# Where the picks of a PEER layer are added: all picks of the second token half in the table matrix, 12 gathered vectors of the first half on VectorE, four table tiles requested before the last dot products

## The chip, the cores and the metric

The kernel runs on one core of one Trainium2 chip. The metric is the device time of one execution in microseconds (us). Engines are called by the profile's names: PE is TensorE, DVE is VectorE, ACT is ScalarE, POOL is GpSimd (here it only issues gathers) and SP is SyncE (here it only issues plain DMAs).

## The reference

A transformer block of 256 tokens with a width of 2048, followed by a second block whose last part is a PEER layer and a final norm. Only that last part matters here:

```
q = (x @ w_q).reshape(B, S, PEER_HEADS, 2, PEER_HALF)          # 8 heads
s = einsum('bshpk,hpnk->bshpn', q, sub_keys)                   # 128 keys on either side
...                                                            # top 16 of the 256 best sums per head
act = gelu(einsum('td,tkd->tk', xt, expert_u[ids])) * g        # 8 x 16 = 128 picks a token
out = einsum('tk,tkd->td', act, expert_v[ids])                 # tables: 16384 experts x 2048
h = h + out ; return rms_norm(h, final_norm_g)
```

## The kernel before

The tokens lie on the 128 partitions, in two halves (t = 0 and t = 1) of 128 tokens. A plan (`Plan`) keeps a rough clock for each engine and writes one list of steps; each engine walks that list and takes its own steps, so it sets the order on each engine. Ahead of the PEER layer lies a stream of projections; the part that the change touches begins at some 2200 us of the run.

**Dots.** For pick n (0 to 127 are those of the first half, 128 to 255 those of the second), POOL gathers one row of `peer_u` a token (`get_u`, L3210, 128 x 8 KB = 1.05 MB) into one of up to six buffers `Ub`, and DVE multiplies and sums it (`dot`, L3071). `U_SETS` says which buffers a pick may use: two leave the ring before the end, and the last 20 dots use `Ub2` to `Ub4`. Each four dots pass a gelu on ACT (L2364) and a product on DVE (`weigh`, L3078), which gives the activations `dots[t]`. Top-k work for the second half lies between the dots of the first.

**Upper 1024 columns of the output.** For the first half, POOL gathers the upper half of a row of `peer_v` for each pick (`get_v`, L3225, 128 x 4 KB = 0.52 MB), ACT makes a diagonal matrix of the activations (L2370) and PE adds the product in the banks M0 and M1 (`spread`, L1920): 128 vectors. 102 of them use a ring of 16384 bytes and one buffer more (`Vx`) or early places (`Vb`), the last 26 four buffers `Vy`. `EARLY_ROWS` lets 106 be requested early; the other 22 come when the dots of pick 236 are due. For the second half, DVE adds the gathered vector times the activation to X (`aside`, L3126): 128 of them.

**Lower 1024 columns.** These go through a dense product with the whole table. For each half, 32 groups (`one_hot`, `spike`, `build`, `keep`) make a 128 x 16384 matrix A[t]: two factors made of one-hot rows, multiplied on PE (`build`, L1943, four products of 128 x 128), copied from the banks T0 and T1 by ACT (`keep`, L2436). The second factor, `spikes`, is made by DVE in four of five groups (L3093) and by ACT in the groups with i % 5 == 1 (L2390, L2393, L2429). In the second half's matrix there are only the first 112 picks (`BUILT`); the last 16 (`LATE`) are added by DVE as 16 more asides of the lower columns, through the indices `vlow`. The last 16 dots are held and lie between the spikes of the second half's matrix, as do the last 22 spreads between the builds.

**Dense stage.** SP loads 128 tiles of `peer_v` (128 rows x 1024 columns, 0.52 MB, L1615), after all spreads, into five places, the fifth free only after the last build. ACT makes a high part (`high`, L2450) and an fp32r copy of the matrix's column (L2456), DVE the low parts of both (L3104, L3111), and PE multiplies (`mul`, L1947, twelve products for a tile). Each eighth tile is not split and goes to PE as fp32, in four products of four passes. The 144 asides lie between the tiles' low parts on DVE. `rows` (L3117) adds M0 and M1 to X, `upper` norms the upper columns, `close` the rest.

Of the kernel before, what the change touches and what calls it, by code (L numbers as in the profile page):

```python
# [15 lines left out]
P = 128  # L16
# [284 lines left out]
class Plan:  # L301
# [642 lines left out]
    def place_free(self, m):  # L944
# [4 lines left out]
        if m >= FIRST_ROWS:  # L949
            return self.when(("chosen", 1, 7)) if NE - 1 in self.spreads else None  # L950
# [42 lines left out]
    def make(self):  # L993
# [22 lines left out]
        yield lambda: None if FIRST_ROWS - 1 not in self.spreads else self.when(("chosen", 1, 7), ("xn", 1, 3))  # L1016
# [6 lines left out]
        yield lambda: self.acted.get(BUILT // GROUP + 31)  # L1023
        self.add("turn_act", 1)
        self.put("ACT", 0.6, self.put("PE", 0.4, 0.0))
        for i in range(32, 64):
            yield lambda: c["ACT"] if on_act(i) else c["DVE"]
            self.add("spike", i)
            self.put("ACT" if on_act(i) else "DVE", 3.3 if on_act(i) else 1.05, 0.0)
            self.build(i)  # L1030
            self.spiked = i - 31
        self.keep(63)

    def products(self):
# [3 lines left out]
        self.spiked = 0  # L1038
# [4 lines left out]
        while self.row_next < 128 or self.ranks.get("weigh", 0) < 256 // GROUP or want:  # L1043
# [18 lines left out]
            if m < 128 and m in self.v_in and m // GROUP in self.acted and m - EARLY_ROWS < 0.75 * self.spiked:  # L1062
# [2211 lines left out]
```

## Time and profile before

| | us |
|---|---|
| runs | 3372.7, 3373.82, 3377.07 |
| median | 3373.82 |
| the profiled execution | 3378.8 |
| its span | 3376.9 |
| dots with full DMA queues, second half | 2600 to 2879 |
| matrix of the second half, with 16 dots and 22 spreads | 2880 to 2965 |
| dense stage, first to last product | 2973.45 to 3364 |
| close | 3364 to 3376.9 |

In a view by stretches, each engine's busy time stands with the number of its instructions in brackets; the last three columns are the clock granted to PE as a share of 2.4 GHz, the busy share of the DMA engines and what they moved. In a list of instructions, the brackets at a row's end say how long the engine stood idle ahead of it and what ended that.

### The profile page before, as it was taken

The page shows a single profiled execution, that of the slowest core. Times are in us where ns is not written, and L with a number is a line of the kernel's source. Part 1 is how long each engine was busy: PE and PEld are TensorE (multiplying, and loading weights), DVE is VectorE, ACT ScalarE, POOL GpSimd, SP SyncE. Part 2 cuts the span into 40 slices and gives each one's busy share as a digit, 9 for nine tenths or more (in the row PEclk, how much of TensorE's full clock was granted, in tenths as well). Part 3 has the DMA queues.
Part 4 walks back from the last instruction along what each step waited for, and adds up shares of the span by engine and source line. Part 5 has one row for each costly group of instructions (what it writes and reads, how often), then busy time and mean ns, then how long its engine had stood idle before and what let it go on. Part 6 is the DMA issues. An engine that isn't in the chain of part 4 may idle for free.

```text
span 3376.9 us, 37646 instructions
## 1 busy us (share of the span) xinstructions
PE 2935.7 (87%) x14064; PEld 2381.0 (71%) x14064; DVE 2590.2 (77%) x3926; ACT 1671.3 (49%) x2698; POOL 597.3 (18%) x549
## 2 busy tenths in 40 slices
PE   8999999999999999999999999986653420789998
PEld 7998998888888888888888888842221320567776
DVE  7786777775557787876557685799889999778987
ACT  6554556554445555554445763133444765444444
POOL 0000000000000000000000000655544333335552
PEclk9999999999999999999999999998876555899999
DMA  6554555555555555556556567999999999889997
GB/s 235 163 150 156 163 170 174 175 163 200 190 182 187 181 192 184 188 181 209 187 188 228 163 203 271 356 380 417 422 403 402 427 427 424 326 325 364 389 369 281
DMA packets 426647, 877.50 MB, mean 260 GB/s; under 512 B 18811, under 2 KB 249116, under 8 KB 392928
## 3 DMA queue, kind: packets, MB, share of 16 engines
q1 hardware_dynamic: 347208, 453.16, 40.3%
q0 software_dynamic: 78240, 421.56, 31.2%
q8 instruction: 112, 1.84, 0.2%
q14 instruction: 71, 0.58, 0.0%
q10 hardware_dynamic: 1016, 0.35, 0.0%
HBM read 872.91 MB, written 2.10 MB: 259 GB/s over the span
## 4 chain that ended last, share of the span: by engine, by line
PE 71%; DMA 12%; DVE 11%; issue 2%; POOL 2%; ACT 2%; DVEq 0%; POOLq 0%; ACTq 0%
PE W L1773 14%; PE W L1781 11%; PE W L1783 11%; PE W L1782 11%; DMA Ub<-in_peer_u,ids 8%; PE W L1771 7%; PE W L1947 7%; DVE Ub L3071 5%; DMA Vr<-in_peer_v 2%; DMA Vx<-in_peer_v,vid 2%; PE M L1920 2%; PE M L1834 1%; DVE X L3126 1%; POOL Ub L3210 1%; PE W L1707 1%
## 5 line engine op out<-in xcount | busy, mean ns | idle before, releaser
L2630 DVE TENSOR_TENSOR wl<-raw,wh 128x1024 fp32r<-128x1024 f32 (+1 forms) x720 | 850.9, 1187 | 562.7 <-ACT wh L2079 561.0
L2079 ACT ACTIVATE wh<-raw 128x1024 fp32r<-128x1024 f32 (+1 forms) x720 | 740.7, 1031 | 893.7 <-PE W L1783 573.9
L1773 PE MATMUL W<-u,wh 128*128 128x512 f32 x2040 | 722.3, 397 | 0.0
L1771 PE MATMUL W<-u,wl 128*128 128x256 f32 x2176 | 603.0, 282 | 0.2 <-DVE u L2592 0.2
L3071 DVE CUSTOM_DVE_ANT_0 Ub<-Ub,W 128x2048 f32<-128x2048 f32 x227 | 516.1, 2284 | 39.1 <-DMA Ub<-in_peer_u,ids 29.3
L1773 PEld LDWEIGHTS W<-u,wh 128*128 128x128 f32 x2040 | 383.3, 188 | 88.2
L1781 PE MATMUL W<-wh,u 128*128 128x512 f32 (+1 forms) x1152 | 436.2, 379 | 1.2 <-DVE u L2990 1.0
L1783 PE MATMUL W<-wh,u 128*128 128x512 f32 (+1 forms) x1152 | 427.9, 371 | 0.0
L1782 PE MATMUL W<-wl,u 128*128 128x512 f32 (+1 forms) x1152 | 427.6, 371 | 0.0
L1771 PEld LDWEIGHTS W<-u,wl 128*128 128x128 f32 x2176 | 410.7, 189 | 6.4 <-issue 0.5
L3210 POOL DMA_INDIRECT Ub<-in_peer_u,ids x256 | 262.0, 1023 | 394.7 <-DVE dots L3071 268.4
L1920 PE MATMUL M<-Vx,diag 128*128 128x512 f32 x360 | 190.3, 682 | 110.7 <-DMA Vx<-in_peer_v,vid 82.5
L1781 PEld LDWEIGHTS W<-wh,u 128*128 128x128 f32 x1152 | 216.5, 188 | 30.7 <-issue 1.4
L1783 PEld LDWEIGHTS W<-wh,u 128*128 128x128 f32 x1152 | 216.2, 188 | 30.6
L1782 PEld LDWEIGHTS W<-wl,u 128*128 128x128 f32 x1152 | 216.6, 188 | 29.0
L1920 PEld LDWEIGHTS M<-Vx,diag 128*128 128x128 f32 x360 | 75.0, 217 | 225.3 <-issue 173.0
L3237 POOL DMA_INDIRECT side<-in_peer_v,vid x128 | 174.7, 1365 | 169.0 <-DVE X L3126 152.5
L1943 PE MATMUL T<-spikes,AA 128*128 128x128 f32 (+1 forms) x512 | 101.2, 363 | 98.2 <-issue 88.3
L3126 DVE SCALAR_TENSOR_TENSOR X<-side,dots,X 128x1024 f32<-128x1024 f32 x144 | 184.3, 1280 | 2.5
L1943 PEld LDWEIGHTS T<-spikes,AA 128*128 128x128 f32 (+1 forms) x512 | 91.5, 265 | 118.7 <-issue 118.7
L1947 PE MATMUL W<-Vh,Ah 128*128 128x512 f32 x448 | 148.0, 411 | 25.4 <-DVE Al L3111 25.3
L3104 DVE TENSOR_TENSOR Vl<-Vr,Vh 128x1024 fp32r<-128x1024 f32 x112 | 137.0, 1223 | 37.9 <-ACT Vh L2450 36.0
(401 smaller groups left out, 4711.4 us busy)
## 6 DMA issues: line engine op xcount, KB each, us to landing
raw<-in_w_in SPq DMA_DIRECT2D x128, 1024.0 KB, 5.2
raw<-in_w_up SPq DMA_DIRECT2D x88, 1024.0 KB, 4.9
Vr<-in_peer_v SPq DMA_DIRECT2D x128, 512.0 KB
raw<-in_w_down SPq DMA_DIRECT2D x44, 1024.0 KB, 5.0
raw<-in_w_in SPq DMA_DIRECT2D x144, 256.0 KB, 3.4
raw<-in_w_out SPq DMA_DIRECT2D x32, 1024.0 KB, 5.0
raw<-in_w_proj_a SPq DMA_DIRECT2D x16, 1024.0 KB, 4.9
Wb<-in_peer_w_q SPq DMA_DIRECT2D x16, 1024.0 KB, 6.7
```

The lines of the kernel that those rows point to most:

```text
L1771: i = q.matmul(pr[h][:, 0:T], vl, xh, start=False, stop=False)
L1773: i = q.matmul(o, vh, u[:, :, kk, :], start=False, stop=last)
L1781: q.matmul(o, th, H[:, k, :], start=first, stop=False)
L1782: q.matmul(o, th, L[:, k, :], start=False, stop=False)
L1783: i = q.matmul(o, tl, H[:, k, :], start=False, stop=last)
L1920: i = q.matmul((M0, M1)[j][:, :], diag[:, m % 4, :], Vb[slot][:, CK[j]], start=m == 0, stop=m == 127)
L1947: return q.matmul(banks[f"W{2 * t + c}"][:, :], left, right, start=j == 0 and k == 0, stop=j == 127 and k == 2)
L2079: q.activation(wh[:, s % NS, 0:b.half], r, ACT.Copy).then_inc(s_hi, 1)
L2630: q.tensor_tensor(wl[:, s % NS, 0:b.half], r, wh[:, s % NS, 0:b.half].bitcast(F32), SUB).then_inc(s_lo, 1)
L3071: q.tensor_tensor_reduce(U[:, :], U[:, :], inputs[:, :], 1.0, 0.0, MUL, ADD, dots[t][:, k:k + 1]).then_inc(s_dot, 1)
L3126: q.scalar_tensor_tensor(X[:, 1, c], side_b[i % NA][:, :], dots[1][:, k:k + 1], X[:, 1, c], MUL, ADD).then_inc(s_aside, 1)
L3210: q.indirect_dma_start(Ub[place][:, :], None, eu, bass.IndirectOffsetOnAxis(ids[t][:, k:k + 1], 0)).then_inc(s_u[place], 16)
```

## The change

The second half's matrix takes all 128 picks (`BUILT`, `LATE` and `vlow` go). The asides of the lower columns go; in their place the first half's last 12 gathered vectors are added by DVE, so that there are 140 asides, 14 of which (`AMID`) lie between the spikes of the second half. PE spreads 116 vectors (`ROWS`), all through the five-place ring, none held. No dot is held either: all 256 lie ahead of the second half's spikes, and the last 20 use four buffers. The ring of spikes has four places instead of six. SP may request four table tiles when 248 dots are done and all picks are chosen. The high and low part of tile 0 lie ahead of the last four builds, and `rows` ahead of the first spike.

```diff
 HALF = D // 2
-LATE = 16
-BUILT = 128 - LATE
 NE = 12
-NB = 4
-FIRST_ROWS = 102
-EARLY_ROWS = 106
+ROWS = 116
...
-ASIDES = 128 + LATE
+ASIDES = 256 - ROWS
+AMID = 14
...
-NP = 6
-U_SETS = ((48, (0, 1, 2, 3)), (206, (0, 1, 2, 3, 4, 5)), (236, (0, 2, 3, 4, 5)), (256, (2, 3, 4)))
+NP = 4
+U_SETS = ((48, (0, 1, 2, 3)), (206, (0, 1, 2, 3, 4, 5)), (236, (0, 2, 3, 4, 5)), (256, (2, 3, 4, 5)))
...
-    if i < 128:
-        return i, 1
-    return BUILT + i - 128, 0
+    return (0, ROWS + i) if i < 128 - ROWS else (1, i - 128 + ROWS)
...
-        yield lambda: self.acted.get(BUILT // GROUP + 31)
+        yield lambda: self.acted.get(63)
         self.add("turn_act", 1)
         self.put("ACT", 0.6, self.put("PE", 0.4, 0.0))
+        self.add("rows")
+        self.put("DVE", 1.3, 0.0)
+        for i in range(ASIDES):
+            self.add("get_aside", i)
...
+            while self.beside < min(AMID, (i - 33) // 2):
+                self.put("DVE", 1.3, 0.0, "aside", self.beside)
+                self.beside += 1
+            if i == 59:
+                self.put("ACT", 1.05, 0.0, "high", 0)
+                self.put("DVE", 1.22, 0.0, "low", 0)
         self.keep(63)
...
-            if dot is not None and n >= 128 + BUILT and self.spiked < 2 * (n - 127 - BUILT):
-                dot = None
...
-            v_free = self.place_free(v) if v < (EARLY_ROWS if n < 124 + BUILT else 128) and v // 16 < self.chosen else None
+            v_free = self.place_free(v) if v < ROWS and v // 16 < self.chosen else None
...
-            while a < min(ASIDES, (j - 1) * ASIDES // 120):
+            while a < min(ASIDES, self.beside + (j - 1) * (ASIDES - self.beside) // 120):
...
-            e.wait_ge(s_spread, 128)
+            e.wait_ge(s_gw, 16)
+            e.wait_ge(s_dot, 248)
             for j in range(128):
                 if j == 4:
                     e.wait_ge(s_built, 64)
```

The last dots on POOL, before: each gather of `peer_u` (`Ub`) has a gather of a vector (`Vy`) near it.

```order
L3225 DMA Vy_271<-in_peer_v,vid_194 128x1024
L3210 DMA Ub_169<-in_peer_u,ids_193 128x2048
L3225 DMA Vy_272<-in_peer_v,vid_194 128x1024
L3225 DMA Vy_273<-in_peer_v,vid_194 128x1024
L3210 DMA Ub_168<-in_peer_u,ids_193 128x2048
```

And now, the last four gathers of `peer_u` and the first asides:

```order
L3202 DMA Ub_168<-in_peer_u,ids_193 128x2048
L3202 DMA Ub_167<-in_peer_u,ids_193 128x2048
L3202 DMA Ub_169<-in_peer_u,ids_193 128x2048
L3202 DMA Ub_170<-in_peer_u,ids_193 128x2048
L3226 DMA side_230<-in_peer_v,vid_194 128x1024
L3226 DMA side_231<-in_peer_v,vid_194 128x1024
```

The 16 gathers are no longer spread through the stage of the second matrix; they lie in one row ahead of it.

On DVE, the start of the second half's spikes, before:

```order
L3078 TENSOR_TENSOR dots_191<-dots_191,gw_185 128x4
L3093 TENSOR_SCALAR spikes_208<-wide_206,idT_202,actT_204 112x128 x4
L3093 TENSOR_SCALAR spikes_209<-wide_206,idT_202,actT_204 112x128 x4
L3071 ISA Ub_167,dots_191<-Ub_167,W 128x2048
L3071 ISA dots_191 128x1
L3093 TENSOR_SCALAR spikes_210<-wide_206,idT_202,actT_204 112x128 x4
```

And now, with the last dot ahead of it:

```order
L3062 ISA Ub_170,dots_191<-Ub_170,W 128x2048
L3062 ISA dots_191 128x1
L3069 TENSOR_TENSOR dots_191<-dots_191,gw_185 128x4
L3108 TENSOR_TENSOR X<-M,X 128x512 x2
L3084 TENSOR_SCALAR spikes_207<-wide_205,idT_201,actT_203 128x128 x4
L3084 TENSOR_SCALAR spikes_208<-wide_205,idT_201,actT_203 128x128 x4
L3084 TENSOR_SCALAR spikes_209<-wide_205,idT_201,actT_203 128x128 x4
L3084 TENSOR_SCALAR spikes_210<-wide_205,idT_201,actT_203 128x128 x4
L3117 SCALAR_TENSOR_TENSOR X<-side_230,dots_190,X 128x1024
```

The dots between the spikes have gone ahead; `rows` and asides have come in.

On PE, the first builds of the second half, before (`T<-spikes` is a build, `M<-Vy` a spread):

```order
L1933 MATMUL T<-ident,dots_191 112x128
L1943 MATMUL T<-spikes_208,AA 128x128 x4
L1920 MATMUL M<-Vy_270,diag 128x512 x2
L1943 MATMUL T<-spikes_209,AA 128x128 x4
L1920 MATMUL M<-Vy_271,diag 128x512 x2
L1943 MATMUL T<-spikes_210,AA 128x128 x4
```

And now:

```order
L1926 MATMUL T<-ident,dots_191 128x128
L1935 MATMUL T<-spikes_207,AA 128x128 x4
L1935 MATMUL T<-spikes_208,AA 128x128 x4
L1935 MATMUL T<-spikes_209,AA 128x128 x4
L1935 MATMUL T<-spikes_210,AA 128x128 x4
L1935 MATMUL T<-spikes_207,AA 128x128 x4
```

No spread is left between the 32 builds.

## Rows read from the trace of the kernel before

**Rows 1.** Stretches: start:end length, busy (count) of PE, PEld, DVE, ACT, POOL; PEclk, DMA, GB/s.
```profile
2600.00:2850.00 250.00, 65.95 (x258) 57.35 (x258) 236.13 (x232) 174.47 (x484) 93.66 (x100) 0.50 1.01 427
2880.00:2965.00 85.00, 73.88 (x345) 48.97 (x345) 62.82 (x139) 43.70 (x112) 34.52 (x37) 0.93 0.85 316
2973.40:3364.00 390.60, 373.62 (x1472) 278.07 (x1473) 346.13 (x370) 166.37 (x244) 190.99 (x139) 0.99 0.93 352
```

**Rows 2.** The same view, three stretches around the end of the first half's dots.
```profile
2530.00:2540.00 10.00, 10.00 (x23) 4.13 (x21) 7.79 (x9) 7.63 (x20) 5.86 (x7) 0.97 0.98 385
2550.00:2560.00 10.00, 0.00 (x0) 0.00 (x0) 9.69 (x22) 3.23 (x8) 1.88 (x3) 0.50 0.91 365
2560.00:2570.00 10.00, 3.18 (x4) 1.51 (x5) 10.00 (x10) 6.84 (x21) 6.74 (x8) 0.50 0.91 334
```

**Rows 3.** Instructions in order of time, POOL: start us, us, engine, line, operation.
```profile
2863.70 0.93 POOL L3225 DMA_INDIRECT Vy<-in_peer_v,vid  x1 [0.30 <-issue]
...
2868.67 0.94 POOL L3210 DMA_INDIRECT Ub<-in_peer_u,ids  x1 [0.30 <-issue]
```

**Rows 4.** The same view, DVE: pick 239's dot and the first spikes.
```profile
2877.02 2.29 DVE L3071 CUSTOM_DVE_ANT_0 Ub<-Ub,W 128x2048 f32<-128x2048 f32 x1 [4.73 <-DMA Ub<-in_peer_u,ids]
...
2880.88 1.38 DVE L3093 TENSOR_SCALAR spikes<-wide,idT,actT 112x128 f32<-112x128 f32 x5 [1.10 <-ACT actT L2384]
```

**Rows 5.** The same view, PE, builds of the second half.
```profile
2882.14 2.04 PE L1943 MATMUL T<-spikes,AA 112*128 112x128 f32 x8 [1.78 <-DVE spikes L3093]
...
2902.07 1.95 PE L1943 MATMUL T<-spikes,AA 112*128 112x128 f32 x16
...
2939.42 1.95 PE L1943 MATMUL T<-spikes,AA 112*128 112x128 f32 x16
...
2944.43 2.05 PE L1943 MATMUL T<-spikes,AA 112*128 112x128 f32 x8 [3.06 <-ACT spikes L2429]
2946.28 2.77 PE L1920 MATMUL M<-Vy,diag 128*128 128x512 f32 x3
```

**Rows 6.** The same view, ACT, around the wait of 3.06 us.
```profile
2940.51 0.60 ACT L2436 ACTIVATE AA<-T 128x512 f32<-128x512 f32 x1 [2.02 <-PE T L1943]
...
2943.06 1.28 ACT L2429 ACTIVATE spikes<-spikes,actT 112x128 f32<-112x128 f32 x4
```

**Rows 7.** Stretches of 2.5 us in which the granted clock changed, and one in which not.
```profile
2885.00:2887.50 2.50, 2.50 (x13) 1.51 (x12) 2.50 (x11) 0.11 (x1) 0.53 (x1) 0.87 0.04 16
2892.50:2895.00 2.50, 1.15 (x10) 0.99 (x10) 2.28 (x10) 2.30 (x7) 1.56 (x2) 1.00 0.91 315
2942.50:2945.00 2.50, 0.57 (x3) 0.60 (x3) 0.00 (x0) 2.47 (x7) 0.00 (x0) 0.74 0.97 357
2950.00:2952.50 2.50, 2.50 (x12) 1.74 (x12) 2.50 (x4) 0.60 (x1) 1.87 (x2) 0.90 0.25 41
2977.50:2980.00 2.50, 2.50 (x12) 2.02 (x11) 1.04 (x2) 0.42 (x1) 0.81 (x1) 0.94 0.40 59
```

**Rows 8.** PE in order of time: the dense stage's first product and two later places.
```profile
2973.45 1.19 PE L1947 MATMUL W<-Vh,Ah 128*128 128x512 f32 x2 [8.49 <-DVE Al L3111]
...
3119.27 0.70 PE L1947 MATMUL W<-Vh,Ah 128*128 128x512 f32 x2 [0.66 <-DVE Al L3111]
...
3132.99 3.59 PE L1947 MATMUL W<-Vr,Ar 128*128 128x512 f32 x8
...
3136.02 1.03 PE L1947 MATMUL W<-Vh,Ah 128*128 128x512 f32 x2
```

**Rows 9.** Who waited for whom, PE in 3000:3364: total us, times, longest.
```profile
PE W L1947 <- DVE Al L3111: 16.5, 14, 2.5
```

**Rows 10.** Groups of DVE, 2965:3377: count, busy us, mean ns, idle before.
```profile
L3126 DVE SCALAR_TENSOR_TENSOR X<-side,dots,X 128x1024 f32<-128x1024 f32 x144 | 184.3, 1280 | 2.5
L3104 DVE TENSOR_TENSOR Vl<-Vr,Vh 128x1024 fp32r<-128x1024 f32 x112 | 137.0, 1223 | 37.9 <-ACT Vh L2450 36.0 <-issue 1.5
L3111 DVE TENSOR_TENSOR Al<-AA,Ah 128x256 fp32r<-128x256 f32 x112 | 46.9, 419 | 5.5 <-ACT Ah L2456 5.2
```

More of the change, by code:

```diff
@@ L155, in landings @@
     count, table = [0] * NE, {}
-    for kind, n, place in ("row", 128, row_sem), ("aside", ASIDES, lambda i: i % NA):
+    for kind, n, place in ("row", ROWS, row_sem), ("aside", ASIDES, lambda i: i % NA):
         for i in range(n):
@@ L1015, in make @@
         self.keep(31)
-        yield lambda: None if FIRST_ROWS - 1 not in self.spreads else self.when(("chosen", 1, 7), ("xn", 1, 3))
+        yield lambda: None if ROWS - 1 not in self.spreads else self.when(("chosen", 1, 7), ("xn", 1, 3))
         self.add("turn_ids", 1)
@@ L1028, in make @@
             self.add("spike", i)
-            self.put("ACT" if on_act(i) else "DVE", 3.3 if on_act(i) else 1.05, 0.0)
+            self.put("ACT" if on_act(i) else "DVE", 3.3 if on_act(i) else 1.15, 0.0)
             self.build(i)
-            self.spiked = i - 31
+            while self.beside < min(AMID, (i - 33) // 2):
[4 more added lines that the diff above has]
+                self.put("DVE", 1.22, 0.0, "low", 0)
         self.keep(63)
@@ L1042, in products @@
         since = 0
[L1043 removed]
+        while self.row_next < ROWS or self.ranks.get("weigh", 0) < 256 // GROUP or want:
             m = self.row_next
@@ L1103, in dense @@
     def dense(self):
-        for i in range(ASIDES):
-            self.add("get_aside", i)
-        a = 0
+        a = self.beside
         for j in range(128):
-            self.add("high", j)
-            self.add("low", j)
-            if j == 0:
-                self.add("rows")
-            while a < min(ASIDES, (j - 1) * ASIDES // 120):
+            if j:
+                self.add("high", j)
+                self.add("low", j)
+            self.add("column", j)
+            while a < min(ASIDES, self.beside + (j - 1) * (ASIDES - self.beside) // 120):
                 self.add("aside", a)
@@ L1421, in program @@
         Vb += [ring_x] + [at(f"Vx{i}", [HALF], END - 16384 + 4096 * i) for i in range(NX - 1)]
-        Vb += [at(f"Vy{i}", [HALF], Z + 16384 + 4096 * i) for i in range(NB)]
         wide_x = ctx.enter_context(nc.psum_tensor("W", [P, D], F32))
@@ L1942, in build @@
                 for x in range(4):
-                    m = q.matmul((T0, T1)[i % 2][:, col(x)], A[t][0:k, g, x * P:x * P + P], spikes[spike_place(i)][0:k, x, :], start=True, stop=True)
+                    m = q.matmul((T0, T1)[i % 2][:, col(x)], A[t][:, g, x * P:x * P + P], spikes[spike_place(i)][:, x, :], start=True, stop=True)
                 m.then_inc(s_built, 1)
@@ L2502, in scalar @@
                   "copy_xn": copy_xn, "top_exp": top_exp, "gelu": gelu, "spread": spread, "turn_ids": turn_ids, "turn_act": turn_act,
-                  "one_hot": one_hot, "spike": spike, "keep": keep_group, "high": high, "upper": upper, "close": close})
+                  "one_hot": one_hot, "spike": spike, "keep": keep_group, "high": high, "column": column, "upper": upper, "close": close})
         def vector(q):
```

92 lines of the change are left out of this document (40 added, 52 removed).

## The prediction

> **What bounds the kernel now.** Only the run behind 2500 us is touched, so I read the view by stretches first. It shows three stages with three bounds [rows 1]. From 2600 to 2850 the DMA engines are full (share 1.01, 427 GB/s) while DVE is busy for 236 of 250 us: the dots come as fast as their rows do. From 2880 to 2965 (second matrix, with 16 dots and 22 spreads among it) DMA falls to 316 GB/s and PE is busy for 74 of 85 us. From 2973.4 to 3364 (dense stage) PE is busy for 373.6 of 390.6 us and DVE for 346. The second view is the list of waits: in the dense stage PE waits 14 times for DVE's `Al`, 16.5 us in all [rows 9]. The third is the list of instructions in order of time, for the paces below.
>
> Two prices recur. A gather of `peer_u` is 128 x 8 KB = 1.049 MB, at 427 GB/s 2.46 us of full DMA; a gathered half row or a table tile is half of that, 1.23 us [rows 1].
>
> **The change, part by part**, in absolute times of the profiled execution.
>
> *Pick 239's dot.* It starts at 2877.02 after a wait of 4.73 us for its row, and ends at 2879.3 [rows 4]. That row was requested at 2868.67, behind four gathers for `Vy`, the first at 2863.70 [rows 3]. The changed order has none there, so I take the whole wait off: 2874.6. The bounds are 0 and 4.7, and it is nearest to the latter, since four times 1.23 us is 4.9.
>
> *Ten more vectors early.* 116 of them go ahead of the second half's dots instead of 106. They are requested between picks 110 and 143, in the neighbourhood of 2530 to 2620, and would cost 10 x 1.23 = 12.3 us if DMA had been full. It was not quite: in three stretches of 10 us it moved 385, 365 and 334 GB/s [rows 2], which leaves (42 + 62 + 93) / 427 x 10 = 4.6 us. I take 7.7 us; bounds 3 (a queue filled at all other places too) and 12.3. ACT's ten diagonals and PE's ten spreads hide there: PE is busy for 66 of 250 us [rows 1]. On POOL each gather waits for the spread five vectors earlier, and gathers of `peer_u` are queued behind it. PE's queue holds a few of these spreads behind first-half builds, which wait for ACT; that is why I don't go below 7.7.
>
> *The 16 dots that were held.* They lose their place in the matrix stage and stand ahead of it, at the pace of DMA: 16 x 2.46 = 39.3 us. DVE's 2.2 to 2.3 us for a dot hides in it. With four buffers, a row has 4 x 2.46 = 9.8 us for its round of request, landing and dot, and the one requested at 2868.67 took 8.35 us to its dot's start while four vectors were in its way [rows 3, 4]; 8.35 + 2.3 is 10.7, without the vectors well below 9.8, so the buffers don't bind. The Trainium skill, "DMA: Bandwidth & Descriptors", section "Anatomy of one DMA — SWDGE (gpsimd) path", fits a lone gather as 2.0 us plus its bytes at 436 GB/s, which is 4.4 us for this one; by it an idle queue would make the round 6.7 us and the sum would be the same. No run here shows a lone one.
>
> *Four tiles early.* SP requests them when 248 dots are done, so they share the DMA engines with the last gathers: 4 x 1.23 = 4.9 us. I take 4, with bounds 0 and 4.9. Together the last dot ends at 2874.6 + 7.7 + 39.3 + 4 = **2925.6**.
>
> *The second matrix, without dots and spreads.* What is late next is ACT. Every fifth group's spikes are made there, and it starts them only after it has copied the group two earlier. The trace shows that pattern once without spreads in the gap: PE starts two builds at 2939.42, ACT copies at 2940.51, its spikes end at 2944.3, and PE starts the next build at 2944.43 after standing idle for 3.06 us [rows 5, 6]. So from the build two groups ahead to the one that waited are 5.0 us. Then three builds lead to the same point of the next round. At full clock they cost 0.9 each (two take 1.95, of which the last 1.06 is one build [rows 5]), some 2.75 with the first; a round is 7.8 us. At half clock the first one takes 1.85 until the next instruction starts (2944.43 to 2946.28 [rows 5]), three 5.5; a round is 10.5.
>
> Which clock is it? In the stretch of that idle the granted clock fell (0.74), and it was back only in the stretch from 2950 (0.90); after an idle of 1.35 us around 2893 it stayed at 1.00 [rows 7]. A mean of 0.87 in the stretch from 2885, 0.90 from 2950 and 0.94 from 2977.5 puts the returns to 2.4 GHz at 2885.6, 2950.5 and 2977.8, so 3.5, 6.1 and 4.3 us after PE had started again at 2882.14, 2944.43 and 2973.45 [rows 5, 7, 8]; mean 4.6. In 4.6 us, 2.5 builds are done at 1.83, and the rest of three takes 0.45: a round is 5.0 + 5.05 = 10.05 us. PE stands idle for 3.06 us in every round now, since nothing fills the gap, so I take this for all. The Trainium skill says in "TensorE: Matmul & The Clock Gate", section "HAM oscillation — how this bites in real kernels", that a loop whose every batch of products waits for its next operand pays the restart at low clock each time and not once; it speaks against this change, the trace agrees in its one such gap, and the other way round (full clock) is a rival below.
>
> The stage then is: last dot to first build 2.8 (2879.3 to 2882.14 [rows 4, 5]) plus `rows`, two adds of some 0.65 = 4.1; two builds and the third's whole 2.05 at half clock, 5.7; copy 0.5, ACT's spikes 3.3: some 13 with the signals, 12.5 if the clock is back for the third. Five rounds (groups 36 to 61) 50.2. From group 61's build to the last copy and through the matrix's first column on ACT and DVE 6.3: builds 4.7, and 1.6 for 0.5 + 0.4 + 0.42 and signals. Sum **69 us**; with all rounds at full clock 12.5 - 1 + 39 + 4.6 = 55, and at half throughout, where the part of 5.0 grows to 5.9, 78. DVE hides: in a round it has four spikes of 1.03 and 2.8 asides of 1.28, 7.7 us.
>
> The first product starts at 2925.6 + 69 = 2994.6. Before it was 2973.45, 8.49 us after PE's last build, waiting for the first tile, its high and its low part [rows 8]. That wait is gone, and it is in the sum: tile 0 is prepared during the builds.
>
> *The dense stage.* For eight tiles DVE has seven pairs of low parts and 9.6 asides (144 over 120 tiles). By busy time, which overlaps by 0.08 from one to the next: 7 x (1.14 + 0.34) + 9.6 x 1.2 = 21.9 us [rows 10]. PE needs 13.72 / 5 = 2.74 for a split tile and 3.03 for an unsplit one, 7 x 2.74 + 3.03 = 22.2 [rows 8]. That tie makes the waits. Afterwards 14 asides are done earlier: 126 are left, 8.4 for eight tiles, DVE 20.4 us. DMA is relieved alike, from 17.6 to 16.4 transfers in eight tiles. PE then bounds alone. The ceiling is the 16.5 us [rows 9], plus what low clock costs: a mean of 0.99 over 390.6 us is up to 8 us at 1.2 GHz, half of it lost, 2.2 of these 4 at the start, where they stay [rows 1, 7]. So 16.5 + 2 = 18.5; I take **18**, and as the other bound 6: DVE relieved by 1.5 us in 22, while waits for late tiles remain (`Vl` waited 36.0 us for ACT's high part [rows 10]). 390.6 - 18 = 372.6, hence 3367.2; the close of 12.9 us stays: 3380.1.
>
> That is 3.2 us more than the span of 3376.9. The profiled execution of 3378.8 would be 3382.0; it lies 5.0 above the median of the runs, 3373.8, so I put the prediction at 3373.8 + 3.2 = **3377.0**.
>
> **The rivals.**
> *PE's clock stays full between the builds.* The stage takes 55 and not 69 us: 3363, faster. For it: the only gap of this kind had its drop, but it is one gap. Against: ACT's order makes the 3.06 us in each round.
> *It stays at half for the whole stage.* Slower: 78 instead of 69 us, 3386. The place is the 32 builds; it decides once the stage takes over 72.6 us, which is when more than some five of the builds that I count at full run at half. For it: first-half builds ran at 0.50 from 2600 on [rows 1]. Against: they had 26% busy PE there.
> *The dense stage gains 6 and not 18.* Its waits come from late tiles and not from DVE's load: 3389.
> *The change doesn't delay the last dot so much*: vectors in gaps (3) and tiles for nothing (0): 3368.
>
> **How the numbers follow.** A measurement of this kernel can tell some 0.2%, 6.7 us. Forecast 0.55, with its own range 3369 to 3385: 0.38 within 6.7 us, 0.12 slower, 0.05 faster. Full clock 0.15, faster. Half clock 0.12, slower. Dense stage 0.10, slower. Earlier last dot 0.08: 0.03 faster, 0.05 the same. Faster 0.23, the same 0.43, slower 0.34. The range reaches from full clock to half clock and nearly to the dense rival: 3362 to 3388.
>
> **What would show it.** The last dot's end near 2926 (below 2920: vectors and tiles were hidden). From there to the first dense product 69 us, and in it six idle times of PE near 3 us with a granted clock between 0.5 and 0.8; a mean near 1.0 proves the first rival. In the dense stage PE's waits for `Al` under 3 us in total and 370 to 375 us from first to last product. The prediction fails if POOL stands for several us behind a spread between 2560 and 2620, or if asides come too late between the spikes, so that DVE's spikes and not ACT's end PE's waits.

## The result and the profile after

The changed kernel takes 3381.9 us (median of 20 runs, 3376.35 to 3385.24); the kernel before, run beside it, 3374.35 us (20 runs, 3371.71 to 3378.29). The ratio is 1.002, with a 95% interval of 1.0014 to 1.0027: slower by 7.5 us or 0.2%, little, but outside the interval of no change. The forecast was 3377.0, 3.2 us slower than before; the time lies within its range. One of the six runs of e10_best_98 below took 13281 us; its ratio leaves that run out, and the median of the other five is 3364.1 us.

The profiled execution took 3378.09 us, with a span of 3376.3. The view by stretches (columns as in [rows 1]) has the stage of the dots, 60 us of the new matrix stage, and the dense stage from its first to its last product:

```profile
2600.00:2850.00 250.00, 72.36 (x275) 57.90 (x275) 231.06 (x228) 176.62 (x491) 95.76 (x102) 0.53 1.01 427
...
2925.00:2985.00 60.00, 37.59 (x251) 35.90 (x252) 49.22 (x125) 37.49 (x87) 17.90 (x19) 0.84 0.54 167
...
2987.60:3365.40 377.80, 370.74 (x1480) 277.17 (x1480) 326.07 (x355) 168.01 (x250) 159.80 (x121) 1.00 0.92 340
```

The first is that of [rows 1] with more spreads on PE. The second is new: PE is busy for 63% of the time, DVE for 82%, and the DMA engines are half idle. No engine is full, so a wait sets the pace. The third is shorter than before. Measured alike, from the first product to the end of the last, the dense stage took 2973.45 to 3366.12 = 392.7 us before and takes 2987.62 to 3365.36 = 377.7 now. (The prediction let it end at 3364 before, two microseconds short; its gain isn't touched by that.)

**The dots.** POOL's instructions in order of time (columns as in [rows 3]) show the first and the last of the last four vectors for PE. They are requested while the first half's dots end and behind them; the dot of pick 128 starts at 2603.45:

```profile
2601.80 1.09 POOL L3214 DMA_INDIRECT Vx<-in_peer_v,vid  x1 [0.30 <-issue]
...
2627.86 0.93 POOL L3214 DMA_INDIRECT Vx<-in_peer_v,vid  x1 [0.31 <-issue]
```

DVE, pick 239's dot (first line; before, [rows 4]) and five of the last eight dots:

```profile
2880.06 2.29 DVE L3062 CUSTOM_DVE_ANT_0 Ub<-Ub,W 128x2048 f32<-128x2048 f32 x1
...
2902.49 2.29 DVE L3062 CUSTOM_DVE_ANT_0 Ub<-Ub,W 128x2048 f32<-128x2048 f32 x1 [0.21 <-DMA Ub<-in_peer_u,ids]
2904.92 2.29 DVE L3062 CUSTOM_DVE_ANT_0 Ub<-Ub,W 128x2048 f32<-128x2048 f32 x1
2907.97 2.29 DVE L3062 CUSTOM_DVE_ANT_0 Ub<-Ub,W 128x2048 f32<-128x2048 f32 x1 [0.75 <-DMA Ub<-in_peer_u,ids]
2911.71 2.29 DVE L3062 CUSTOM_DVE_ANT_0 Ub<-Ub,W 128x2048 f32<-128x2048 f32 x1 [1.44 <-DMA Ub<-in_peer_u,ids]
...
2924.59 2.29 DVE L3062 CUSTOM_DVE_ANT_0 Ub<-Ub,W 128x2048 f32<-128x2048 f32 x1
```

Up to 2904.92 they stand 2.4 to 2.6 us apart, the time of their rows at 427 GB/s. SP issues the four tiles at 2902.35, and the next five each come 3.05 to 3.74 us after the one ahead. The last one ends at 2926.9.

**The matrix.** PE in order of time, from the first build to the first dense product (before, [rows 5, 8]):

```profile
2929.69 5.66 PE L1935 MATMUL T<-spikes,AA 128*128 128x128 f32 x32 [1.77 <-DVE spikes L3084]
2938.38 4.95 PE L1935 MATMUL T<-spikes,AA 128*128 128x128 f32 x40 [3.03 <-ACT spikes L2419]
2946.27 6.45 PE L1935 MATMUL T<-spikes,AA 128*128 128x128 f32 x40 [2.94 <-issue]
2955.66 4.95 PE L1935 MATMUL T<-spikes,AA 128*128 128x128 f32 x40 [2.94 <-issue]
2963.55 6.45 PE L1935 MATMUL T<-spikes,AA 128*128 128x128 f32 x40 [2.94 <-issue]
2972.94 3.93 PE L1935 MATMUL T<-spikes,AA 128*128 128x128 f32 x32 [2.94 <-issue]
2979.94 1.13 PE L1935 MATMUL T<-spikes,AA 128*128 128x128 f32 x8 [3.07 <-DVE spikes L3084]
2981.37 4.50 PE L1935 MATMUL T<-spikes,AA 128*128 128x128 f32 x24 [0.30 <-issue]
2987.62 0.70 PE L1939 MATMUL W<-Vh,Ah 128*128 128x512 f32 x2 [1.75 <-DVE Al L3102]
```

Eight instructions are one build; x40 are the five of a round. There are the six idle times near 3 us that the prediction named. Five of them stand ahead of a group whose spikes ACT makes. The sixth, at 2979.94, is another: it stands behind DVE, which waited for ACT's high part of tile 0 (below), and the last group of ACT's, at 2981.37, waits for 0.30 us only. The rounds alternate: from build to build of the same place they take 7.89 and 9.39 us. Two stretches of the first view, a short round and the long one behind it, tell why (the granted clock is the column after the busy times: 1.00, then 0.82). The last two stretches lie in the long round, the first 0.8 us of its builds and what follows:

```profile
2938.40:2946.30 7.90, 4.96 (x41) 4.70 (x41) 7.68 (x19) 6.04 (x15) 2.76 (x3) 1.00 0.64 196
2946.30:2955.70 9.40, 6.46 (x41) 6.25 (x41) 7.26 (x20) 6.03 (x15) 1.92 (x3) 0.82 0.47 124
2946.27:2947.07 0.80, 0.80 (x7) 0.80 (x8) 0.13 (x1) 0.38 (x1) 0.08 (x1) 1.00 0.27 20
2947.10:2950.50 3.40, 3.40 (x18) 3.40 (x17) 2.31 (x5) 1.20 (x2) 0.37 (x1) 0.51 0.48 152
```

The clock is full during the pause and when PE starts again. It falls 0.8 us later, with PE at work, and PE works through the whole stretch at half clock: five builds take 6.45 us and not 4.95. The last three builds are slow too (4.50 us, against 2.96 at full clock in e3).

ACT in such a round: a copy, its spikes in three steps, and the next copy only behind them (compare [rows 6]):

```profile
2942.35 0.60 ACT L2426 ACTIVATE AA<-T 128x512 f32<-128x512 f32 x1 [0.30 <-PE T L1935]
2942.84 1.26 ACT L2381 ACTIVATE spikes<-wide,idT 128x128 f32<-128x128 f32 x4
2944.14 0.72 ACT L2384 ACTIVATE spikes<-spikes,wide 128x512 f32<-128x512 f32 x1
2944.89 1.28 ACT L2419 ACTIVATE spikes<-spikes,actT 128x128 f32<-128x128 f32 x4
2946.07 0.57 ACT L2426 ACTIVATE AA<-T 128x512 f32<-128x512 f32 x1
```

PE's build at 2946.27 starts when the spikes are done (2944.89 + 1.28 = 2946.17). Where the list names "issue", I read the same signal behind it, by these times.

DVE's wait behind the sixth idle time:

```profile
2977.59 1.23 DVE L3095 TENSOR_TENSOR Vl<-Vr,Vh 128x1024 fp32r<-128x1024 f32 x1 [3.73 <-ACT Vh L2439]
```

**The dense stage.** Who waited for whom, over the whole of it, and then one of DVE's groups from 3000 to 3364, columns as in [rows 10]:

```profile
PE W L1939 <- DVE Al L3102: 8.7, 11, 2.0
```

```profile
L3095 DVE TENSOR_TENSOR Vl<-Vr,Vh 128x1024 fp32r<-128x1024 f32 x107 | 131.0, 1224 | 41.9 <-ACT Vh L2439 41.4
```

In the stretch of [rows 9] the waits were 16.5 us in 14 times; they are 6.9 in 10 now.

### The profile page after: what moved, and what is told of

Its sections match the earlier page's. It is cut to its first block, busy times and chain, and to the rows that moved or that the text cites. A ratio compares the mean times of both kernels' runs of the same rounds, so it can differ in the third digit from the quotient of the medians.

```text
span 3376.3 us, 37505 instructions
## 1 busy us (share of the span) xinstructions
PE 2907.4 (86%) x14016; PEld 2369.3 (70%) x14016; DVE 2586.4 (77%) x3921; ACT 1667.3 (49%) x2686; POOL 563.2 (17%) x533
## 4 chain that ended last, share of the span: by engine, by line
PE 73%; DMA 13%; DVE 9%; issue 2%; ACT 1%; POOL 1%; DVEq 0%; ACTq 0%; POOLq 0%
PE W L1767 14%; PE W L1775 11%; PE W L1777 11%; PE W L1776 11%; DMA Ub<-in_peer_u,ids 9%; PE W L1939 8%; PE W L1765 7%; DVE Ub L3062 5%; DMA Vx<-in_peer_v,vid 2%; PE W L1701 2%; DMA Vr<-in_peer_v 2%; PE M L1828 1%; PE T L1935 1%; PE M L1914 1%; PE W L1764 1%
## 5 line engine op out<-in xcount | busy, mean ns | idle before, releaser
L1914 PE MATMUL M<-Vx,diag 128*128 128x512 f32 x416 | 221.1, 685 | 148.7 <-DMA Vx<-in_peer_v,vid 122.4
L1914 PEld LDWEIGHTS M<-Vx,diag 128*128 128x128 f32 x416 | 86.8, 218 | 280.3 <-issue 187.7
L1935 PE MATMUL T<-spikes,AA 128*128 128x128 f32 x512 | 98.3, 364 | 99.1 <-issue 80.0
L3117 DVE SCALAR_TENSOR_TENSOR X<-side,dots,X 128x1024 f32<-128x1024 f32 x140 | 178.9, 1278 | 0.8
L1935 PEld LDWEIGHTS T<-spikes,AA 128*128 128x128 f32 x512 | 89.5, 267 | 109.3 <-issue 108.9
```

The source lines that it names most:

```text
L1914: i = q.matmul((M0, M1)[j][:, :], diag[:, m % 4, :], Vb[slot][:, CK[j]], start=m == 0, stop=m == ROWS - 1)
L1935: m = q.matmul((T0, T1)[i % 2][:, col(x)], A[t][:, g, x * P:x * P + P], spikes[spike_place(i)][:, x, :], start=True, stop=True)
```

## The experiments

Each ratio is to the kernel before, run beside it on the same chip; its medians were 3375.71, 3375.67 and 3376.68 us for e1 to e4, e5 to e8 and e9 to e12. (e1 to e4 ran on another chip than the rest, but the kernel before took the same on both.) Edits are to the changed kernel. The stage is from the last dot's end to the first dense product, the dense stage to the end of its last product, both in the profiled execution (in e3 the extra products are left aside).

| kernel | median us | ratio, 95% | last dot | stage | dense |
|---|---|---|---|---|---|
| changed | 3381.9 | 1.0014 to 1.0027 | 2926.9 | 60.7 | 377.7 |
| e1_all_dve | 3377.63 | 0.9992 to 1.001 | 2927.1 | 57.9 | 378.3 |
| e2_split | 3371.35 | 0.9969 to 0.9991 | 2926.4 | 50.6 | 376.5 |
| e3_fill | 3379.07 | 0.9998 to 1.0016 | 2928.0 | 59.1 | 379.4 |
| e4_tiles_256 | 3374.02 | 0.9985 to 1.0002 | 2924.4 | 61.1 | 377.4 |
| e5_again | 3379.23 | 1.0003 to 1.0021 | 2926.9 | 60.9 | 376.6 |
| e6_best | 3365.16 | 0.9959 to 0.998 | 2923.7 | 51.9 | 376.5 |
| e7_amid0 | 3388.53 | 1.0025 to 1.0052 | 2928.9 | 62.7 | 385.1 |
| e8_rows106 | 3372.79 | 0.9983 to 1.0001 | 2912.8 | 63.9 | 380.0 |
| e9_best_106 | 3355.24 | 0.9928 to 0.9953 | 2907.4 | 50.3 | 380.7 |
| e10_best_98 | 3364.6 | 0.9954 to 0.9979 | 2904.2 | 50.9 | 392.8 |
| e11_high_54 | 3380.45 | 1.0005 to 1.0022 | 2928.1 | 61.1 | 378.4 |
| e12_small_asides | 3370.93 | 0.9975 to 0.9992 | 2926.5 | 60.8 | 367.6 |

The theory for the first experiments, as the profile after suggests it: ACT's spikes hold up its copies and pace the builds (A); the rival is that DVE paces them (B). The same kernel gave 3381.9 and 3379.23 us in two sets of runs, so differences of medians under 3 us decide nothing here; the traces do. A trace is one execution: in the ten kernels with 116 vectors on PE, pick 239's dot starts between 2879.16 and 2881.64, so differences of under 2.5 us in such a time decide nothing either. The stage repeats better: it takes 60.7 to 61.1 us in the changed kernel, e4, e5, e11 and e12.

### e1_all_dve: no spikes of the second half on ACT

```
-    return i < 32 or i % 5 == 1
+    return i < 32
```

> The changed kernel with all 32 spike groups of the second half made on DVE; ACT only copies there. Theory A (ACT's order bounds the stage: a group's spikes of 3.3 us delay a copy, and PE stands for 3 us in each round, losing its clock): the pauses of 3 us of PE go, DVE then bounds with 32 x 1.03 + 14 x 1.2 + rows 1.2 + one low part 1.2 = 52 us, and from the last dot's end (2926.9 in the changed kernel's trace) to the first dense product it takes 56 to 58 us and not 60.7; 2 to 6 us faster than the changed kernel, 3376 to 3380. Theory B (DVE's spikes and asides already end PE's waits): 6 more groups on DVE make the stage longer by 6 x 1.03 = 6 us, 3388.

PE's builds come in pairs at an even pace, one pair in 3.28 us, each behind DVE (PE in order of time, two of ten such lines):

```profile
2941.90 2.02 PE L1935 MATMUL T<-spikes,AA 128*128 128x128 f32 x16 [1.25 <-DVE spikes L3084]
2945.18 2.02 PE L1935 MATMUL T<-spikes,AA 128*128 128x128 f32 x16 [1.25 <-DVE spikes L3084]
```

Five groups take 8.2 us instead of a mean of 8.6. The pauses near 3 us ahead of ACT's groups are gone, so ACT's spikes do make them. But DVE is nearly as late: giving it all the spikes replaces one bound by the other and gains 3 us.

### e2_split: ACT's spikes in three pieces

```
-            self.add("spike", i)
-            self.put("ACT" if on_act(i) else "DVE", 3.3 if on_act(i) else 1.15, 0.0)
+            if not on_act(i):
+                self.add("spike", i)
+                self.put("DVE", 1.15, 0.0)
+            for part in range(3):
+                x = i + 2 - part
+                if x < 64 and on_act(x):
+                    self.add("spike_part", x, part)
+                    self.put("ACT", (1.3, 0.75, 1.3)[part], 0.0)
```

> The changed kernel with ACT's spikes cut into three pieces (1.26, 0.72 and 1.28 us) that lie one group apart, so that each of ACT's copies is delayed by one piece alone. Same work, another order on ACT. Theory A: no pause of PE is over 1.5 us, the granted clock stays at 1.00 once it has risen, and five groups take DVE's 4 x 1.03 + 2.5 x 1.2 = 7.1 us in place of 7.9 to 9.4: the stage falls from 60.7 to about 52 us, 8 to 10 us faster than the changed kernel, 3372 to 3374. Theory B: DVE bounds either way, under 2 us.

The three steps are the same instructions, with a copy between each two (ACT, then PE, in order of time):

```profile
2939.11 1.27 ACT L2436 ACTIVATE spikes<-wide,idT 128x128 f32<-128x128 f32 x4
2940.28 0.58 ACT L2451 ACTIVATE AA<-T 128x512 f32<-128x512 f32 x1
2940.76 0.72 ACT L2440 ACTIVATE spikes<-spikes,wide 128x512 f32<-128x512 f32 x1
```

```profile
2943.22 3.93 PE L1941 MATMUL T<-spikes,AA 128*128 128x128 f32 x32 [1.08 <-ACT spikes L2444]
2947.67 1.13 PE L1941 MATMUL T<-spikes,AA 128*128 128x128 f32 x8 [0.52 <-ACT AA L2451]
2949.88 3.93 PE L1941 MATMUL T<-spikes,AA 128*128 128x128 f32 x32 [1.08 <-ACT spikes L2444]
```

A round is 6.66 us, the stage 10.1 us shorter than the changed kernel's, the median 7.9 us below e5_again. That is theory A: ACT does as much work as in the changed kernel, and so does DVE; only the order on ACT differs. The 10.1 us hold the clock as well: from 2936 to 2977 it is granted at 1.00, also behind the one pause near 3 us that is left (3.28 us ahead of 2970.82, behind DVE and tile 0).

### e3_fill: the pauses filled with products

```
+FILL = 3
...
+                if i >= 32 and on_act(i):
+                    e.wait_ge(s_dot, 256)
+                    for _ in range(FILL):
+                        q.matmul(banks["W0"][:, :], ident[:, :], X[:, 1, 0:512], start=True, stop=True)
```

> The changed kernel with three more fp32 products of 128 x 512 on PE ahead of each build whose spikes ACT makes, into a bank that nobody reads before it is started anew; they add nothing to the output. At full clock they take 2.6 us and lie in the pause of 3 us. If the low clock costs what I said (a round of five groups 7.9 us at full clock and 9.4 when it has dropped, both seen in the trace): all six rounds take 7.9 us, 2 to 5 us faster than the changed kernel in the median, 3377 to 3380. If the pauses alone cost and the clock does not: the same or up to 3 us slower.

```profile
2944.99 2.74 PE L1934 MATMUL W<-X,ident 128*128 128x512 f32 x6
2948.10 4.94 PE L1940 MATMUL T<-spikes,AA 128*128 128x128 f32 x40 [0.37 <-issue]
...
2955.99 4.95 PE L1940 MATMUL T<-spikes,AA 128*128 128x128 f32 x40 [0.37 <-issue]
```

```profile
2946.30:2955.70 9.40, 8.95 (x50) 6.04 (x48) 8.35 (x23) 7.51 (x19) 2.81 (x3) 1.00 0.50 156
```

Where the changed kernel was granted 0.82, this one has 1.00, and each of the four rounds takes 7.89 us. So idle time of PE is what costs the long rounds their 1.5 us, and a round at full clock lasts 7.89 whatever PE does: ACT's order sets it. The two long rounds give back 3.0 us, but the stage gains only 1.6 to 1.8 us: its first group of ACT's comes 0.7 us later than in the changed kernel (9.4 and 8.7 us from the first build), and its end is 0.6 us longer, where the extra products delay group 61's build. The median gains nothing that can be told, against 2 to 5 us expected.

### e4_tiles_256: the four tiles after the last dot

```
-            e.wait_ge(s_dot, 248)
+            e.wait_ge(s_dot, 256)
```

> The changed kernel with the four table tiles requested when all 256 dots are done, not 248. Theory A: the last dots are 2.46 us apart again and not 3.05 to 3.74, the last one ends 4.9 us earlier (2922 and not 2926.9), and nothing is late behind it, since tile 0 isn't needed for another 45 us: 4 to 5 us faster than the changed kernel, 3377. Rival: the tiles then collide with the first gathers for DVE's adds, which come later by as much: the same as the changed kernel, 3382.

```profile
2919.70 2.29 DVE L3062 CUSTOM_DVE_ANT_0 Ub<-Ub,W 128x2048 f32<-128x2048 f32 x1 [0.17 <-DMA Ub<-in_peer_u,ids]
2922.14 2.29 DVE L3062 CUSTOM_DVE_ANT_0 Ub<-Ub,W 128x2048 f32<-128x2048 f32 x1
```

The last dots keep their 2.45 us. From the start of pick 239's dot to the last dot's start are 40.5 us, in the changed kernel 44.5: the tiles cost 4.0. (The last dot ends only 2.5 us earlier, since pick 239's started 1.6 later in this execution.) The stage behind it isn't longer than the changed kernel's (61.1 and 60.7 us), so the tiles cost nothing there; the DMA share from 2925 to 2985 is 0.61 here. The median is 5.2 us below e5_again.

### e5_again: the changed kernel once more

> The changed kernel itself, once more, beside the three others. Its trace of before had rounds of five groups of 7.9 and 9.4 us in turn. If the granted clock's falls depend on where in the round the pause of 3 us lies, another execution shows another pattern (rounds between 7.9 and 10.5) with the same order of instructions, and its stage from last dot to first dense product lies between 58 and 68 us (60.7 before); if the pattern is fixed by the program, it is 60.7 again within 1 us. Ratio to the kernel before 1.002.

The same pattern: rounds of 7.89 and 9.40 us, the stage 60.9. The ratio is 1.0012 here and was 1.002; the two intervals overlap.

### e6_best: pieces, late tiles, and tile 0's high part five groups earlier

```
-            if i == 59:
+            if i == 54:
                 self.put("ACT", 1.05, 0.0, "high", 0)
+            if i == 59:
                 self.put("DVE", 1.22, 0.0, "low", 0)
...
-            e.wait_ge(s_dot, 248)
+            e.wait_ge(s_dot, 256)
```

(and e2's edit)

> Three edits together: ACT's spikes in three pieces (as in the second experiment), the four tiles requested at 256 dots (as in the fourth), and ACT's high part of tile 0 laid five groups before DVE's low part of it, since both traces show DVE and then PE standing for 3 us there (PE waits 3.07 and 3.28 us for DVE's spikes). If the three are independent: 10 to 14, 4 to 5 and 2 to 3 us less than the changed kernel, 16 to 22 in all, 3360 to 3366, 8 to 14 us faster than the kernel before. If the early high part collides with ACT's pieces: no gain from the third, 3364 to 3368.

Faster than before by 2 to 4 in 1000. The gain of 6.2 us over e2 is about that of the tiles; the stage, 51.9 us, gained nothing from the third edit.

### e7_amid0: no asides among the builds

```
-AMID = 14
+AMID = 0
```

> The changed kernel with no asides between the spikes: all 140 lie in the dense stage (AMID 0), as 144 did in the kernel before. Tests why the dense stage is shorter (375.8 in place of 390.6 us). If it is DVE's and the DMA engines' load there: 140 asides bring most of PE's waits back (16.5 us in the kernel before, 6.9 in the changed one), the dense stage takes 385 to 390 us; the stage of the builds hardly gets shorter, since ACT's order bounds it and not DVE, by 0 to 4 us; in all 5 to 12 us slower than the changed kernel, 3387 to 3394. If the dense stage is shorter because of the earlier start of its tiles: 376 to 378 us, no slower than the changed kernel.

The stage is not shorter without them (62.7 us), and a round at full clock takes 7.89 us here too (2949.40 to 2957.29), so DVE's asides did hide in it. The dense stage has 140 instead of 126 and takes 7.4 us more. By the medians the 14 asides between the builds are worth 9 us to the changed kernel.

### e8_rows106: the old split of the vectors in the new order

```
-ROWS = 116
+ROWS = 106
```

> The changed kernel with 106 vectors on PE and 150 asides on DVE, so that as many vectors lie ahead of the second half's dots as in the kernel before. Tests the price of the ten vectors. By my sum they delay the last dot by 7.7 us (bounds 3 and 12.3): it ends near 2919. Ten more asides in the dense stage, 136 in place of 126, cost there a part of what they hold of DVE: 10 x 1.2 = 12 us of work, of which some 4 to 8 show as PE's waits. In all 0 to 4 us faster than the changed kernel. If the ten vectors were hidden in gaps: the last dot ends within 3 us of 2927 and the kernel is 4 to 8 us slower.

POOL's last request of a vector for PE, and DVE's dot of pick 239:

```profile
2543.07 1.00 POOL L3214 DMA_INDIRECT Vx<-in_peer_v,vid  x1 [0.30 <-issue]
```

```profile
2865.98 2.29 DVE L3062 CUSTOM_DVE_ANT_0 Ub<-Ub,W 128x2048 f32<-128x2048 f32 x1 [0.17 <-DMA Ub<-in_peer_u,ids]
```

Pick 239's dot starts 14.1 us earlier than with 116 vectors (2880.06). Ten gathers at full price are 12.3, and the expectation had 7.7. In return the dense stage is 2.3 to 3.4 us longer. The stage is 3.2 us longer too, because of the clock: here two long rounds follow each other (PE in order of time), three of four are long, and the builds ahead of and behind them are slow as well:

```profile
2925.07 6.42 PE L1935 MATMUL T<-spikes,AA 128*128 128x128 f32 x40 [2.77 <-issue]
2934.57 6.45 PE L1935 MATMUL T<-spikes,AA 128*128 128x128 f32 x40 [3.07 <-ACT spikes L2419]
```

By the medians ten vectors more on PE cost 6.4 us on balance.

### e9_best_106 and e10_best_98: the version that the runs point to

e6's edits with `ROWS = 106`, and with `ROWS = 98`.

> The kernel of e6_best (spikes in three pieces, tiles after dot 256, tile 0's high part at group 54) with 106 instead of 116 vectors added by PE, so 150 by VectorE. Theory A, the prices add: ten gathers fewer ahead of the last dot give back 13 to 14 us there, as in e8_rows106, and 136 instead of 126 asides make the dense stage some 2 to 5 us longer. Last dot's end near 2910, first dense product near 2963, median 3356 to 3360. Theory B, the ten asides need gaps that the shorter matrix stage no longer has, and fall behind in the dense stage: last dot as above, but PE's waits for Al over 15 us in the dense stage and a median above 3363.

> As e9_best_106 with 98 vectors for PE and 158 for VectorE; 144 asides are then left for the dense stage, as many as in the kernel before. Eight gathers at 1.23 us less ahead of the last dot: 9.9 us earlier than e9. Theory A, linear as from 116 to 106: the dense stage takes 2 to 3 us more, median 6 us below e9. Theory B, VectorE binds the dense stage at 144 asides (21.9 against 22.2 us for eight tiles): it takes some 388 us, 9 to 10 us more than e9, and the median is e9's within 3 us; PE's waits for Al near 16 us.

Views by stretches of the two dense stages (e9, e10):

```profile
2957.70:3338.50 380.80, 369.65 (x1480) 275.78 (x1480) 337.69 (x365) 168.76 (x250) 181.17 (x131) 1.00 0.93 352
2955.00:3347.80 392.80, 372.42 (x1480) 276.96 (x1480) 348.28 (x373) 168.13 (x250) 199.99 (x139) 1.00 0.93 351
```

In them PE waits for `Al` 13 times in e9, 12.8 us in all, and 19 times in e10, 22.1 us.

e9 is the fastest kernel of this study, 21 us below the one before (ratio 0.994). The prices added, as its theory A had it, and a little more: by the medians of e2, e4 and e8 against e5_again one would have 7.9 + 5.2 + 6.4 = 19.5 us below e5_again, and e9 is 24.0 below it. e10 went by its theory B: its dense stage took 392.8 us, as long as that of before with its 144 asides (392.7). The last dot came only 3.3 us earlier than e9's, not 9.9. Most of that shows at the end of the first half's dots (the view by stretches, e9, then e10):

```profile
2540.00:2570.00 30.00, 7.07 (x12) 2.84 (x12) 29.38 (x54) 10.42 (x26) 11.29 (x12) 0.68 1.01 425
2540.00:2570.00 30.00, 0.00 (x0) 0.00 (x0) 29.52 (x49) 9.56 (x25) 8.66 (x10) 0.50 0.84 320
```

In e9 the DMA engines are full there. In e10, with eight vectors fewer, they move 320 GB/s, which is (425 - 320) / 427 x 30 = 7.4 us unused, and DVE is busy for 29.5 of 30 us. POOL waits there ten times for one of DVE's dots to free a buffer, 22.9 us in all. So the vectors taken away left room that nothing could fill, since DVE set the pace.

### e11_high_54: tile 0's high part earlier, alone

e6's edit at groups 54 and 59, without the others.

> The changed kernel, with one task moved: ACT makes the high part of tile 0 at group 54 and not at group 59. Theory A, VectorE stood behind it with its low part: PE's idle time of 3.07 us behind VectorE's spikes near the end of the builds goes, the first dense product comes some 3 us earlier, median 3 us below e5_again (3376 us). Theory B, ACT's own order makes up for it (its spikes for groups 56 and 61 start 1 us later): no more than 1 us gained.

DVE doesn't wait for tile 0's high part now (in the changed kernel it waited 3.73 us for it, and PE 3.07 behind that):

```profile
2975.31 1.15 DVE L3096 TENSOR_TENSOR Vl<-Vr,Vh 128x1024 fp32r<-128x1024 f32 x1
```

But PE stands as long for ACT's spikes, and the stage takes 61.1 us:

```profile
2975.01 6.33 PE L1936 MATMUL T<-spikes,AA 128*128 128x128 f32 x40 [3.48 <-ACT spikes L2420]
2984.40 3.04 PE L1936 MATMUL T<-spikes,AA 128*128 128x128 f32 x24 [3.06 <-ACT spikes L2420]
```

Theory B: that wait was in the shadow of ACT's.

### e12_small_asides: what DVE's load costs the dense stage

```
+                to = D if i < 14 else HALF + 256
...
-                q.scalar_tensor_tensor(X[:, t, HALF:D], side_b[i % NA][:, :], dots[t][:, k:k + 1], X[:, t, HALF:D], MUL, ADD).then_inc(s_aside, 1)
+                q.scalar_tensor_tensor(X[:, t, HALF:to], side_b[i % NA][:, 0:to - HALF], dots[t][:, k:k + 1], X[:, t, HALF:to], MUL, ADD).then_inc(s_aside, 1)
```

> The changed kernel; from aside 14 on VectorE multiplies and adds 256 of an aside's 1024 columns only (the other columns of these vectors are left out of the output). Gathers, waits and their order are as before, so that VectorE alone is relieved, by some 0.8 us for each of 126 asides. Theory A, VectorE's load makes PE's remaining waits for Al (6.9 us in the dense stage): they fall below 2 us and the dense stage to 369 to 371 us, median 5 us below e5_again. Theory B, the waits come with late tiles (DMA share 0.94 to 0.99): they stay within 2 us of 6.9, and the dense stage at 374 to 376 us.

The aside falls from 1278 to 479 ns (groups of DVE, 3000 to 3364), and DVE now stands still for ACT's high parts:

```profile
L3095 DVE TENSOR_TENSOR Vl<-Vr,Vh 128x1024 fp32r<-128x1024 f32 x107 | 131.1, 1226 | 112.2 <-ACT Vh L2439 111.8
L3118 DVE SCALAR_TENSOR_TENSOR X<-side,dots,X 128x256 f32<-128x256 f32 x122 | 58.4, 479 | 0.8
```

```profile
PE W L1939 <- DVE Al L3102: 3.0, 2, 1.7
```

The dense stage takes 367.6 us, of which PE is busy for 366.3, so with PE's present work it can hardly be shorter. The changed kernel's is 10.1 us longer with the same transfers. Of these, 5.7 us are waits for `Al` (8.7 and 3.0), the price of DVE's work on the asides. (The smaller asides also read and write less; this edit doesn't separate that from DVE's time.) The other 4.4 are PE's busy time for the same 1480 products. Some 1.6 of them are half clock behind a wait of 2.01 us up to 3059.72. That need not be DVE's doing: e6, e7 and e9 have a wait of 2.0 us in the dense stage and no half clock behind it. The other 2.8 are open.

## Why the prediction was right in sum, and where its steps failed

The span was forecast as 3380.1 and was 3376.3. By its terms:

| term | predicted | measured |
|---|---|---|
| end of pick 239's dot (2874.6 + 7.7) | 2882.3 | 2882.35 |
| 16 dots and four tiles | 43.3 | 44.5 |
| stage | 69 | 60.7 |
| gain of the dense stage | 18 | 15.0 |

3380.1 + 1.3 - 8.3 + 3.0 = 3376.1: the terms account for the span to 0.2 us.

*Pick 239 and the ten vectors.* The sum is right by luck: two errors cancel. The vectors cost 14.1 us (e8), not 7.7. My upper bound of 12.3 was the nearer value, and even it was short: pick 239's dot starts at 2879.16 to 2881.64 in the ten kernels with 116 vectors, and at 2865.54 and 2865.98 in the two with 106. I read the room in stretches around 2550 [rows 2]. But that room belonged to the order of before: from 2550 to 2570, e8 moves 425 GB/s with no more vectors than before, which moves 350 there. And the last four vectors were requested at 2601.80 to 2627.86, where DMA moves 427 GB/s and there is no room. The price isn't the same for each vector either: e10's eight fewer gave 3.2 us at pick 239. The second error: the new order at 106 vectors gave 11.0 us at pick 239 (2877.02 before, 2865.98 in e8), not the 4.7 of the one wait that I saw in [rows 4]. The rest had come earlier: the request of pick 110's row is at 2535.50 before and 2532.33 in e8, of pick 130's at 2590.70 and 2585.32. The room from 2550 to 2570, (425 - 350) / 427 x 20 = 3.5 us, is part of it. The request of pick 80's row is already 2.8 us earlier (2420.52 and 2417.68); why is open.

*16 dots and tiles.* Right: 40.5 us (e4) and 4.0 against 39.3 and 4.

*The stage.* Its three parts were predicted as 12.5, 50.2 and 6.3 us, and measured as 11.5 (2926.88 to 2938.38), some 43 (to group 61's build, near 2981.4) and 6.2. The mechanism was right: e2 shows that ACT's order makes the pauses, and e3 that PE's idle time costs the clock. The round at full clock was predicted as 7.8 and is 7.89. What failed is the step "I take this for all": the granted clock fell in every second round only (in e8 in three of four), and then cost 1.5 us (9.39 - 7.89), not 2.25. I had one such gap in the trace, and made a rule of it. The 2.25 came from counting PE's work at half clock from its restart to the clock's return, 4.6 us. The return was near that, 4.3 us behind the restart at 2946.27, but the first 0.8 us of it ran at full clock. The sixth pause was behind DVE's low part of tile 0, for which my sum had no wait; with ACT's own pause for group 61 in its shadow (e11), that cost nothing. The truth lay between my forecast and the rival of the full clock, which was closer (55 us). The Trainium skill, in "TensorE: Matmul & The Clock Gate", section "HAM oscillation — how this bites in real kernels", has the restart paid for each batch; here the changed kernel paid it in two rounds of four.

*The dense stage.* "PE then bounds alone" failed. PE waited 8.7 us for `Al` and not under 3, and e12 shows that DVE's load made it wait, though by my sum DVE needs 20.4 us for eight tiles where PE needs 22.2. A sum over eight tiles may hide that an aside of 1.28 us stands between a tile's `Vl` and its `Al` at the moment when PE comes to it; that is argued, not shown. The other part of the gain goes with the clock, as I had it: PE's busy time for the same 1480 products fell from 375.7 to 370.7 us. With PE's busy time x (1 - granted clock) summed over stretches of 2.5 us, half clock cost 5.6 us before and 1.6 now, so that 4.0 of the 5.0 are the clock. Each stretch at half clock, other than at the stage's start, lies behind one of the longest waits: 2.04 us up to 3048.24 and 2.50 up to 3270.03 before, 2.01 up to 3059.72 now. So part of this gain hangs on the waits too, but not each wait of 2 us has it (e6, e7 and e9 have none at half clock).

*From span to median.* This step failed as well. The forecast of 3377.0 lies within 5 us of the median only since its span was 3.8 us too long. I put the median 5.0 us below the profiled execution, as it was before. But the profile of before was above all 20 runs that later stood beside the changed kernel's (up to 3378.29), and that of after is the third from below among its 20. So the traces differ by -0.6 us, the medians by +7.5 (by +3.6 in e5). The mean granted clock of each run was noted: at 0.927 the changed kernel took 3382.0 to 3384.1 us, at 0.930 3376.4 to 3379.8. Perhaps the slower runs lose it at more of the six pauses; that would fit with 1.5 us for each and with e8's two long rounds in a row. But it is not shown, and e3, without most of the pauses, spread as widely (3373.7 to 3382.8). It stays open.

*The rivals.* Full clock: refuted for every second round. Half throughout: refuted (0.84 from 2925 to 2985). Its 78 us isn't written out; by its parts (five rounds of 5.9 + 5.5 between the 13 and some 7 us) I get 77. Dense stage gains 6: refuted. An earlier last dot: refuted, 2926.9.

## What to carry to other kernels

A step that runs on a second engine only to relieve the first can delay what that engine does for everybody; look at what stands behind it in order, and cut it in pieces before moving it away (10 us here, for no work less). Where two engines feed each other tile by tile, a sum with room to spare is not enough to say that nobody waits, and the price of an extra piece of work rises as the room fills (here from 0.3 to 1.9 us). Price a transfer at the place where it will be issued, and look whether the room that a trace shows there belongs to the order that the change takes away.

## What the runs showed of the hardware that was not expected

- After pauses of the same length, 2.94 us, in the same sequence of builds, the granted clock of the following round was 1.00 and 0.82 by turns. In e5 the rounds alternate alike, in e8 two slow ones stand in a row. The fall didn't come in the pause but 0.8 us after PE had started again (1.00 in 2946.27:2947.07, 0.51 in 2947.10:2950.50, with PE busy throughout). With the pauses filled by 2.74 us of products no round was slow.
- In the dense stage a wait of 2.0 us was followed by half clock in the changed kernel, in e1 and in e5, and not in e6, e7 and e9. e10 had waits of 2.31 us (up to 3251.37), with half clock behind it, and of 2.58 us (up to 3130.32), without. Among the builds of e2, 3.28 us ahead of 2970.82 left it at 1.00. By the length of a pause alone the fall can't be foretold.
- The dense stage against the number of asides left for it: 126 give 376.5 to 379.4 us in eight traces, 136 give 380.0 and 380.7, 140 give 385.1 and 144 give 392.7 (before) and 392.8 (e10). The first ten cost some 0.3 us each, the last four 1.9.
- Tiles of 0.52 MB requested among gathers delay them by most of their bytes' time at 427 GB/s: four cost 4.0 us, against 4.9 worked out from bytes.
